# Latent attention of the prompt with keys and values expanded per head, and the residual gains on GpSimd

## The reference, cut to what matters

```python
def mla_project(x, pos, w_in, q_norm, kv_norm, w_uq, w_uk):
    cq, ckv, kr = jnp.split(x @ w_in, [256, 384], axis=-1)
    cq, ckv = rms_norm(cq, q_norm), rms_norm(ckv, kv_norm)
    kr = rope(kr[:, :, None, :], pos)[:, :, 0]
    q = (cq @ w_uq).reshape(B, S, 8, 64 + 32)
    q_nope, q_rope = jnp.split(q, [64], axis=-1)
    q_lat = jnp.einsum('bshn,chn->bshc', q_nope, w_uk)      # 128 wide per head
    return q_lat, rope(q_rope, pos), concatenate([ckv, kr])

def mla_attend(q_lat, q_rope, rows, mask):
    s = einsum('bqhc,bkc->bhqk', q_lat, ckv) + einsum('bqhr,bkr->bhqk', q_rope, kr)
    p = softmax(where(mask, s * 96 ** -0.5, -1e30))
    return einsum('bhqk,bkc->bqhc', p, ckv)

def mla_output(ctx, w_uv, w_out):
    o = jnp.einsum('bqhc,chv->bqhv', ctx, w_uv).reshape(B, S, 8 * 64)
    return o @ w_out
```

## Time and profile before

| | |
|---|---|
| Median of 3 runs | 1032.1 us (1026.12 to 1035.33) |
| Span of the profiled execution | 1029.5 us |
| Time of the profiled execution beside its span | not listed |
| Mean granted clock of TensorE | 0.975 of full |
| PE busy | 964.9 us, 94% |
| PE weight loads busy | 596.7 us, 58% |
| DVE busy | 512.0 us, 50% |
| ACT busy | 357.9 us, 35% |
| POOL busy | 246.0 us, 24% |

### The profile page before, as it was taken

One profiled execution on the slowest core, in us unless ns is written; L12 is line 12 of the kernel. 1 busy time (PEld: TensorE's weight loads), 2 busy tenths in 40 slices (PEclk: granted clock), 3 DMA queues, 4 the chain that ended last, 5 costly groups with the idle time before them and its releaser, 6 DMA issues.

```text
span 1029.5 us, 17722 instructions
## 1 busy us (share of the span) xinstructions
PE 964.9 (94%) x6944; PEld 596.7 (58%) x6944; DVE 512.0 (50%) x1071; ACT 357.9 (35%) x894; POOL 246.0 (24%) x291
## 2 busy tenths in 40 slices
PE   7999999998998998899999998999899979999995
PEld 6876787888444856433334766657648654333332
DVE  0245530376748678333222555784188783323227
ACT  3335532020001534234333353655214542443323
POOL 3550000052500012555210016400000025552130
PEclk9999999999999998899999999999999987999998
DMA  9836101172206166899999504441237166999977
GB/s 319 193 108 227 42 1 34 49 205 82 72 0 172 43 283 220 293 353 418 412 418 397 195 22 99 90 155 42 74 132 286 42 241 206 351 415 414 417 210 179
DMA packets 78060, 203.61 MB, mean 198 GB/s; under 512 B 19128, under 2 KB 44384, under 8 KB 68880
## 3 DMA queue, kind: packets, MB, share of 16 engines
q1 hardware_dynamic: 61568, 153.44, 40.8%
q0 software_dynamic: 16400, 48.93, 15.3%
HBM read 184.46 MB, written 25.92 MB: 204 GB/s over the span
## 4 chain that ended last, share of the span: by engine, by line
PE 73%; DVE 13%; DMA 6%; ACT 4%; issue 3%; POOL 1%; SPq 0%; DVEq 0%; POOLq 0%; ACTq 0%
PE PS L1658 15%; PE PS L1445 10%; PE PS L1088 9%; PE PS L1675 7%; PE PS L1192 6%; PE PS L1476 3%; DMA x<-y_tok 2%; PE PS L1646 2%; ACT arena L2064 2%; PE PS L1111 2%; DMA arena<-in_moe_w_in_dram 2%; PE PS L1916 2%; PE PS L1072 1%; PE PS L1906 1%; PE PS L1153 1%
## 5 line engine op out<-in xcount | busy, mean ns | idle before, releaser
L1658 PE MATMUL PS<-ring,arena 128*32 128x512 f32 x696 | 137.6, 592 | 0.5 <-DMA arena<-in_moe_w_in_dram 0.5
L2064 ACT ACTIVATE arena<-PS 32x520 f32<-32x520 f32 (+9 forms) x155 | 76.7, 505 | 176.1 <-PE PS L1088 43.0
L1658 PE MATMUL PS<-arena 128*32 128x512 f32 x600 | 108.4, 605 | 2.0 <-issue 2.0
L1088 PE MATMUL PS<-xT,ring 128*128 128x260 f32 x416 | 95.2, 390 | 4.3 <-DVE arena L2566 3.1
L3154 DVE COPY arena<-PS 128x256 f32<-128x256 f32 x24 | 10.2, 425 | 173.6 <-PE PS L1666 173.6
L1088 PEld LDWEIGHTS PS<-xT,ring 128*128 128x128 f32 x416 | 79.5, 193 | 19.1 <-DVE arena L2566 5.1
L2363 ACT ACTIVATE arena<-PS,lnc 128x128 f32<-128x128 f32 x184 | 66.9, 468 | 38.0 <-PE PS L1646 38.0
L1658 PEld LDWEIGHTS PS<-ring,arena 128*32 128x32 f32 x696 | 37.1, 110 | 55.1 <-issue 50.2
L848 POOL TENSOR_TENSOR rstd<-rstd,small 128x1 f32<-128x1 f32 (+1 forms) x20 | 13.5, 675 | 225.2 <-DVE rstd L2854 225.2
L1675 PE MATMUL PS<-ring,arena 128*32 128x512 f32 x408 | 65.4, 595 | 0.6 <-DVE arena L3154 0.6
L1192 PE MATMUL PS<-ring,xT 128*128 128x256 f32 (+2 forms) x336 | 65.2, 354 | 0.0
(11 more groups left out here) (444 smaller groups left out, 1833.7 us busy)
## 6 DMA issues: line engine op xcount, KB each, us to landing
ring<-in_moe_w_in_dram SPq DMA_DIRECT2D x29, 1024.0 KB, 11.7
arena<-in_moe_w_in_dram SPq DMA_DIRECT2D x25, 1024.0 KB, 10.5
ring<-in_moe_w_out_dram SPq DMA_DIRECT2D x17, 1024.0 KB, 11.4
ring<-in_w_in_even_dram SPq DMA_DIRECT2D x11, 1024.0 KB, 12.3
xT<-in_moe_w_in_dram SPq DMA_DIRECT2D x10, 1024.0 KB, 11.5
arena<-in_moe_w_out_dram SPq DMA_DIRECT2D x9, 1024.0 KB, 11.0
xT<-in_moe_w_out_dram SPq DMA_DIRECT2D x6, 1024.0 KB, 13.7
y_tok<-in_c_zeros_dram POOLq DMA_DIRECT2D x8, 512.0 KB, 11.1
```

Of the source, the lines that this page charges most:

```text
L1088: mm = pe.matmul(o[out_rows, 512 * h:512 * h + HALF], lhs(k), rhs(k)[:, HALF * h:HALF * h + HALF], start=(k == 0), stop=(k == nk - 1))
L1658: mm = pe.matmul(o[group(q), 0:512], xT_[:, k, group(q)], w(q, k), start=(k == 0), stop=(k == KD - 1), **quarter(q))
L2064: return act.activation(dst, src, ACT.Copy)
```

## The change

The prompt part of the attention no longer works in the latent space. Keys are expanded once: `kn` is the product of `w_uk` with the latents, two heads to 128 rows, 512 columns. Values too: `vt` is latents times `w_uv`, a tile of 128 tokens by 512 columns, kept in the back part of `xT`. The main score of a head is then a product of 64 rows, with two heads on rows 0 to 63 and 64 to 127. The apply gives 64 columns per head, two products of 128 columns per key tile, straight into `oT`. Samples stay absorbed: their eight `ql` products have 8 columns each and are done after the second score, with the transposes of their rotary parts and six ACT copies; their value projection has 8 columns per head. The filler products in this stage go. `natr` moves out of `xT`. DVE's ten gains go to POOL, behind its page requests, by the function that it has.

```diff
 def latent_steps(n):
-    out = [("S", 0), ("S", 1)]
+    out = [("S", 0), ("S", 1), ("samples", 0)]
...
-             ("oin", 3), ("oinT", 2), ("oin", 4), ("ukT",), ("qn", 0), ("oinT", 3), ("qn", 1), ("oinT", 4)]
+             ("oin", 3), ("oinT", 2), ("oin", 4), ("ukT",), ("qn", 0), ("oinT", 3), ("kn", 0), ("oinT", 4), ("qn", 1)]
+LATENT_QUERIES = keys("""qn.2 qn.3 qrope.0 kn.1 qrope.1 qrT.0 vt.0 qrope.2 qrT.1 vt.1 qrope.3 qrT.2 qrope.4 qrT.3""")
...
-        q_lat = part(8, T)
-        ctxT = q_lat
+        knT = part(4, SEQ)
+        natr = part(2 * D)
+        ctx_s = part(8, DB)
...
-        natr = x_flat[:, 0:2 * D]
+        v_lat = x_flat[:, v_at:v_at + 2 * D].rearrange("p (t n) -> p t n", t=4)
...
                     for b in range(SP_REQUESTS, DB):
                         request_pages(pool, b, "late_pages_in")
+                    for t in range(NT):
+                        gains(2, t)
                     pool.wait_ge(s["x_ready"], NT * 2)
...
+                def head_keys(i):
+                    key = ("kn", i)
+                    o = open_(key)
+                    landed(pe, ("uk",))
+                    taken(pe, ("oinT", 3))
+                    for j in range(2):
+                        c = 2 * i + j
+                        mm = pe.matmul(o[:, 512 * j:512 * j + SEQ], wview(("uk",))[:, c * P:c * P + P], ckvT[:, 0:SEQ], start=True, stop=True)
+                    close(mm, key)
+                def head_values(i):
+                    key = ("vt", i)
+                    o = open_(key)
+                    landed(pe, ("uv",))
+                    for j in range(2):
+                        mm = pe.matmul(o[:, 512 * j:512 * j + 512], ckvT[:, tile_cols(2 * i + j)], wview(("uv",))[:, :], start=True, stop=True)
+                    close(mm, key)
...
-                    if t == 4:
-                        unread_products(o[:, 896:1024], 10)
...
-                for h in range(8):
-                    key = ("ql", h)
-                    open_(key)
-                    b, c = 64 * (h % 2), h // 2
-                    close(by_feature(key, lambda k: ukT[b:b + 64, c, :], lambda k: qnT[b:b + 64, c, :], 1), key)
...
-                unread_products(pair(("qrT", 4))[:, 896:1024], 6)
...
+                def sample_latents(_):
+                    key = ("ql",)
+                    o = open_(key)
+                    taken(pe, ("ukT",))
+                    for h in range(8):
+                        b, c = 64 * (h % 2), h // 2
+                        mm = pe.matmul(o[:, 512 * (h % 2) + DB * c:512 * (h % 2) + DB * c + DB], ukT[b:b + 64, c, :], qnT[b:b + 64, c, 512:520], start=True, stop=True)
+                    close(mm, key)
+                    q_rope_back(4)
...
                 def score(i, o, blk):
                     n, h0, g, w = blk
                     o = o.rearrange("p (g w) -> p g w", g=g)
+                    taken(pe, ("qrT", n))
                     for h in range(h0, h0 + g):
-                        pe.matmul(o[:, h - h0, 0:w], q_lat[:, h, n * P:n * P + P], ckvT[:, 0:w], start=True, stop=False)
+                        b, c = 64 * (h % 2), h // 2
+                        pe.matmul(o[:, h - h0, 0:w], qnT[b:b + 64, c, n * P:n * P + P], knT[b:b + 64, c, 0:w], start=True, stop=False)
...
                 def apply(i, o, blk, v):
                     n, h0, g, w = blk
+                    taken(pe, ("vt", n // 2))
                     for c in range(n + 1):
-                        mm = pe.matmul(o[:, 0:g * P], rows[:, c, 0:P], v[:, c, :, :], start=(c == 0), stop=(c == n))
+                        for h in range(h0, h0 + g):
+                            b = 64 * (h % 2)
+                            mm = pe.matmul(o[b:b + 64, 0:P], v_lat[:, c, 64 * h:64 * h + 64], v[:, c, h - h0, :], start=(c == 0), stop=(c == n))
...
-                for j in range(4):
-                    key = ("uv", j)
...
+                key = ("uv",)
+                o = open_(key)
+                for h in range(8):
+                    b, c = 64 * (h % 2), h // 2
+                    mm = pe.matmul(o[b:b + 64, DB * c:DB * c + DB], wview(("uv",))[:, 64 * h:64 * h + 64], ctx_s[:, h, :], start=True, stop=True)
+                close(mm, key)
...
-                        take(att_key(kind, "O", i), ctxT[:, h0:h0 + g, tile_cols(n)],
-                             lambda o: o[:, 0:g * P].rearrange("p (g q) -> p g q", g=g))
+                        take(att_key(kind, "O", i), oT[:, h0 // 2, tile_cols(n)], lambda o: o[:, 0:P])
...
+                def samples():
+                    act.wait_ge(s["qrS_zero"], 1)
+                    full(act, ("ql",))
+                    for par in range(2):
+                        ins = copy(qlS[:, :, par:8:2], pair(("ql",))[:, 512 * par:512 * par + 32].rearrange("p (c b) -> p b c", c=4))
+                    free(ins, ("ql",))
+                    full(act, ("qrT", 4))
+                    for q in range(4):
+                        ins = copy(qrS[32 * q:32 * q + 32, q, :, 0:8], pair(("qrT", 4))[32 * q:32 * q + 32, 0:64].rearrange("p (h b) -> p b h", h=8))
+                    free(ins, ("qrT", 4))
...
-                def gains(i):
-                    if i == GAIN_BLOCKS:
-                        dve.wait_ge(s["ln_in"], 32 * 3)
...
-                latent_blocks(gains)
+
+                latent_blocks()
```

More of the change, by code:

```diff
@@ L336, in decoder_step @@
         else:
[L337 removed]
+            piece(("uk",), io["w_uk"][0].rearrange("c h n -> c (h n)"), (512,), ("kn", 1))
             for i in range(2):
@@ L774, in memory_cache @@
                 if l:
-                    full(sp, ("uv", 3))
+                    full(sp, ("uv",))
                     sp.wait_ge(s["rows_out"], 16 * NT)
@@ L1125, in attention @@
             def attention(kind, score, apply, order, between=None):
-                steps = {**attention_steps(kind, score, apply), "W": between}
+                steps = {**attention_steps(kind, score, apply), "W": between, "samples": between}
                 for st_, i in order:
@@ L2219, in sliding_attention, with latent_blocks @@
                     outputs(i)
-            def latent_blocks():
+            def latent_blocks(samples):
                 exps, probs_turned, outputs = attention_steps("mla")
@@ L2224, in latent_blocks @@
                 exps(0)
+                samples()
                 for i in range(n):
@@ L2470, in latent_attention @@
                     steps[key[0]](*key[1:])
-                act.activation(st[0:1, 26:27], small[0:1, EPSILON:EPSILON + 1], ACT.Exp)
-                act.wait_ge(s["moe_done"], 1)
-                for j in (1, 3):
-                    take(("qn", j), halves(qnT[:, j, :]), halves)
-                for h in (1, 3, 5, 7):
-                    take(("ql", h), halves(q_lat[:, h, :]), halves)
-                for t in range(4):
-                    take(("qrT", t), qrT2[:, :, tile_cols(t)], lambda o: o[:, 0:256].rearrange("p (c q) -> p c q", c=2))
-                taken(act, ("ql", 6))
-                taken(act, ("ql", 7))
-                act.wait_ge(s["qrS_zero"], 1)
-                copy(qlS[:, :, 0:8], q_lat[:, :, 512:520].rearrange("p h b -> p b h"))
-                full(act, ("qrT", 4))
-                for q in range(4):
-                    ins = copy(qrS[32 * q:32 * q + 32, q, :, 0:8], pair(("qrT", 4))[32 * q:32 * q + 32, 0:64].rearrange("p (h b) -> p b h", h=8))
-                free(ins, ("qrT", 4))
-                act.wait_ge(s["moe_done"], 1)
-                latent_blocks()
+                    if key == ("oinT", 4):
+                        act.activation(st[0:1, 26:27], small[0:1, EPSILON:EPSILON + 1], ACT.Exp)
+                        act.wait_ge(s["moe_done"], 1)
+                def samples():
[8 more added lines that the diff above has]
+                    free(ins, ("qrT", 4))
+                latent_blocks(samples)
                 for g in range(2):
@@ L2516, in latent_attention @@
                 for i in range(2):
-                    ins = copy(ctxT[:, :, 512 + 4 * i:516 + 4 * i].rearrange("p h b -> p b h"),
+                    ins = copy(ctx_s[:, :, 4 * i:4 * i + 4].rearrange("p h b -> p b h"),
                                pair(key)[:, i * P:i * P + P].rearrange("p (b h) -> p b h", b=4)[:, :, 0:8])
                 free(ins, key)
-                for j in range(4):
-                    take(("uv", j), halves(oT[:, j, :]), halves)
+                take(("uv",), oT[:, 0:4, 512:520], lambda o: o[:, 0:32].rearrange("p (c b) -> p c b", c=4))
             act.wait_ge(s["lnc_in"], 16 * 2)
@@ L2644, in sliding_attention, with latent_blocks @@
                     between(i + 1)
-            def latent_blocks(between):
+            def latent_blocks():
                 maxima, scale = attention_steps("mla")
@@ L2653, in latent_blocks @@
                     scale(i)
-                    between(i)
             n_rows = [0]
@@ L3241, in latent_attention @@
                 dve.wait_ge(s["moe_done"], 1)
```

(19 more changed lines are left out.)

70 lines of the change are left out of this document (30 added, 40 removed).

## The result

The changed kernel took 1036.62 us (median of 18 runs, 1029.21 to 3333.14, the last one disturbed), against 1031.34 us for the kernel before in the same session (18 runs, 1024.92 to 1037.4). The ratio is 1.0052, with a 95% interval of 1.0031 to 1.0073: half a per cent slower, where 1026 was forecast.

A forecast was written before the change was run, and what follows sets the result against it. PE was taken to bound the attention. Tail 3.3, ramp 1.5 and blocks 10.7 gave 15.5 us, 1029.5 to 1014, or 1016.6 on the median; 9.7 for DVE waiting on POOL made 1026.3, forecast 1026, range 1014 to 1038.

The forecast's parts named there:

- two turns: Attention blocks beside POOL's gains: DVE waits two POOL turns per block, 5.4 us; cost 9.7 us, chance 0.45.
- third rival: Same blocks: negated maximum and both scalings each wait, 8.1 us per block; cost 16.5, so 1033 us; chance 0.17.
- A turn: One POOL gain of 2.38 us plus 0.3 for its gap and the DVE operation let in: 2.7 us.
- the ramp: Attention's start, up to about 650 us: earlier first score and mask, less sample copies; gain 1.5 us (0 to 3).
- the fourth rival: Clock falls to 1.2 GHz during two or three turns: 2.3 us on five blocks, 11.5, so 1038 us; chance 0.10.
- The sum without waits: Whole kernel without new waits: 15.5 us gained, 1029.5 to 1014 us, or 1016.6 on the median.
- the tail: Attention's end, value projection to next matmul: 4.47 us falls to 1.2; gain 3.3 us (3.0 to 3.6).
- single scores and applies: Attention blocks: narrower scores save 5.2 us and applies 5.5 us, 10.7 in all.
- the halves overlap: 64-row scores of two heads run together, 1.07 instead of 1.72 us at 512 columns; no-overlap rival had chance 0.03.
- the expert stall: Wait for expert weights, 16.83 us: moves along with the rest, neither growing nor shrinking.
- POOL's own queue: Ten gains behind POOL's page requests end near 692 us, before x_ready is wanted past 735: no cost there.
- DVE as the next bound: Widest blocks: with gains left on DVE it would cost 4.1 us, level with PE's 4.2.

The follow-up runs named there:

- e1: The changed kernel with the ten gains put back on DVE: 1023.59 us, ratio 0.9926.
- e5: The kernel before with only its 16 unread products taken out, products left full-height: 1034.15 us, ratio 1.0034.
- e4: The kernel before with only the ten gains moved to GpSimd: 1043.61 us, ratio 1.0096.
- e9: The changed kernel with gains on DVE, samples' products just before the last apply, and full-height unread products (7, then 2 per block) in blocks 0 to 7: 1015.96 us.
- e13: e9 with the ten gains on GpSimd, whole and placed as in the change: 1029.23 us, ratio 0.9981.
- e7: The changed kernel with gains on DVE and the samples' work moved to just before the last apply, no unread products: 1024.34 us, ratio 0.9957.
- e3: e1 plus 14 unread products ahead of the transposes of blocks 0 to 3: 1027.16 us, ratio 0.9893.
- e8: The changed kernel with the samples' work just before the last apply and GpSimd's gains started after that apply: 1027.99 us, ratio 0.9976.
- e2: The changed kernel plus 14 unread products ahead of the transposes of blocks 0 to 3, gains still on GpSimd: 1034.75 us, ratio 1.0023.
- e14: e9 with narrow unread products (64 rows, 8 columns; 12, then 3 per block) instead of full-height ones: 1037.2 us, ratio 1.0051.

## Why the prediction was wrong

**The failed steps.** The forecast was 1016.6 without waits, plus 9.7 for two turns. Two things went otherwise. *Turns per block:* there were three, as the third rival had it. The negated maximum waited and the two scalings went in one at a time. A turn was 2.4 us (7.21 per block), not 2.7, and four intervals took 27.3 us instead of 14.2 in e1, so the cost was about 13 and not the rival's 16.5. *The clock:* the forecast tied a fall to the turns, gave it 0.10, and let the early blocks run at full clock for nothing. It fell in the ramp, before GpSimd had begun, once the change had removed the full-height unread products (e5 shows that this is enough), and it stayed down for 20 us, twice as long as in e5; that the narrower products make the difference is likely but not shown by itself. That cost 6 to 7. In the turns the clock fell as well, as the fourth rival had it (0.50 from 674 to 690), but that was hidden: the maxima are 7.21 us apart there and 7.27 in e4 (683.24 to 690.51), where the clock read 1.00 from 682 to 690 us. The ramp had given a warning: 0.54 after a stretch of 0.27 busy us was read for the turns, and not for the ramp from which the fillers were taken.

That 1036.62 lies inside the range of 1014 to 1038 is luck. The upper end came from the fourth rival, 11.5 us for a clock that falls in the turns; there it cost nothing, and three turns and the ramp took its place. A smaller slip: the price of the two turns sets five blocks at 3.1 and 4.0 us, where the paragraph before had 3.2 and 4.2; with those the cost would have been 9.0 instead of 9.7. And the multiply of 0.41 us at 273.88, taken for the free time, starts itself while POOL's four operations run (268.00 to 276.05), so those rows didn't show when an operation is held.

**The two add up.** The four corners, by median and ratio:

| | clock kept (e9's ramp) | clock lost (the change's ramp) |
|---|---|---|
| gains on DVE | 1015.96, 0.986 (e9) | 1023.59, 0.9926 (e1) |
| gains on POOL | 1029.23, 0.9981 (e13) | 1036.62, 1.0052 (changed) |

By the medians POOL costs 13.3 and 13.0 us and e9's ramp is worth 7.6 and 7.4; by the ratios it is 12.5 and 13.0, and 6.8 and 7.3. e9's ramp differs from the change's in two things, the place of the samples and the unread products. Neither alone kept the clock in its profile (e7, e3), though some executions of e3 kept it by their times; and e9's 21 unread products with the samples in the change's place were not tried.

**What held.** The sum without waits, 15.5 us, or 1016.6 on the median: e9, which has the expanded attention and neither loss, measured 1015.96 against 1030.31, 14.4 less, though it also has 21 unread products and the gains on DVE. That this is near 15.5 is in part luck: in e9's profile, with a span 16.2 us shorter than before, the ramp gained 5.0 us where 1.5 was forecast, the blocks up to the sixteenth maximum 4.6, the tail 3.5, and 3.0 lie behind the start of the output projection, where the change gives no reason for them. The single scores and applies were sized right, the halves overlap, the tail gained 3.5 where 3.3 was forecast, the expert stall moved along, POOL's own queue held nobody up. The ramp gained more than forecast: 3.6 us by the first maximum, 5.0 counted against the transposes of x before it. The sum without waits, 1016.6, plus the 12.8 and the 7.0 of the table of maxima makes 1036.4; that this is near the measured 1036.62 is no proof, since the 12.8 is counted against blocks with the gains on DVE (14.6 against e8's 24.14) and the ramp gained 3.5 more than the sum has.

**DVE as the next bound.** Level with PE, as forecast, it cost little: wide blocks with the gains on DVE (25.96) are 1.8 us longer than without a gain beside them (24.14 in e8).

## What to carry to other kernels

Before moving elementwise work to GpSimd, list the SBUF-to-SBUF operations that VectorE has on the path in that stretch, tiny ones too (the reciprocal was exempt here), and charge each one whole GpSimd instruction; if the work must go there, cut its instructions short. When unread products are removed, or products made narrower, look at the granted clock of the stretch after it, at PE busy 100% as well: a busy PE may be one at half speed. Run the two-by-two when two losses are suspected, since a single repair here was worth little (e2) or looked like the whole story (e1).

## What was not expected of the hardware

- The granted clock fell to 0.50 with PE recorded as busy 2.00 of 2.00 us in every stretch (e14), and once down stayed there for 20 us (changed kernel) to 43 us (e3) in which PE never paused, mostly in 64-row and 32-row products; with mostly full-height ones it was back after some 10 us (e5).
- A DVE operation of 128 x 2 elements took 0.93 us instead of 0.17, and in e4 2.32, beside GpSimd instructions that it had nothing to do with; the reciprocal of the same 128 x 2 elements kept its 0.15.
- GpSimd's instruction of 128 x 256 takes 0.75 us where 128 x 1024 takes 2.34 to 2.46: the quarters cost 25% more in all, and still gained 9.9 us.
